# Gated convolutions ahead of the last column sums, a second norm, group choice and sort in fewer steps, and a shared down product behind the first gate-up, in a mixer and mixture-of-experts block

## What is computed

```python
mod = c @ w_ada + b_ada;  sh1, sc1, g1, sh2, sc2, g2 = split(mod, 6)      # column sums of w_ada, 1024 x 6144
h = modulate(rms_norm(x, norm_mix_g), sh1, sc1)                           # x: 256 tokens x 1024
cb, cc, cu, z, xbc, dt_raw = split(h @ w_in)
y_a = cb * causal_dwconv(cc * cu, conv_a_w)                               # the gated convolutions, 512 channels
y_b = ssd_mixer(z, xbc, dt_raw, ...)                                      # Mamba-2, 8 heads, ends in its own rms_norm
x = x + g1 * (concat([y_a, y_b]) @ w_out)
h = modulate(rms_norm(x, norm_ffn_g), sh2, sc2)                           # the second norm
scores = sigmoid(h @ w_router);  sel = scores + router_bias               # 64 experts in 8 groups of 8
# per token: a group's score is the sum of its two best; 4 groups stay; the 8 best experts in them are taken
out = (silu(h @ ws_gate) * (h @ ws_up)) @ ws_down                         # the shared expert
for e in range(64):
    out += gates[:, e:e+1] * ((silu(h @ we_gate[e]) * (h @ we_up[e])) @ we_down[e])
return rms_norm(x + g2 * out, norm_final_g)
```

## Time and profile before

| what | value |
|---|---|
| median of 3 runs | 698.68 us |
| lowest and highest | 696.64 and 699.54 us |
| the profiled execution, own time | 698.76 us |
| its span, first to last instruction | 697.0 us |
| mean granted clock of PE | 0.971 |
| PE busy | 628.4 us (90%) |
| DVE busy | 256.5 us (37%) |
| ACT busy | 124.2 us (18%) |
| moved from HBM | 248.9 MB |

### The profile page before, as it was taken

One profiled execution on the slowest core, in us unless ns is written; L12 is line 12 of the kernel. 1 busy time (PEld: TensorE's weight loads), 2 busy tenths in 40 slices (PEclk: granted clock), 3 DMA queues, 4 the chain that ended last, 5 costly groups with the idle time before them and its releaser, 6 DMA issues.

```text
span 697.0 us, 11733 instructions
## 1 busy us (share of the span) xinstructions
PE 628.4 (90%) x4453; PEld 347.2 (50%) x4453; DVE 256.5 (37%) x705; ACT 124.2 (18%) x269; POOL 43.3 (6%) x225
## 2 busy tenths in 40 slices
PE   3699999789986999999899999998899999999892
PEld 0288878534544445454344454552445455544440
DVE  0167939774374133141323231231233121432115
ACT  2311220201310111111111211110111111111113
POOL 7000000000201000001000000010000001000000
PEclk9999999969999999999999999998999999999997
DMA  8998893652429999999999999999999999999941
GB/s 345 380 402 337 332 397 135 276 223 93 181 106 415 411 423 421 422 420 418 421 421 419 421 420 421 420 421 420 420 420 419 420 421 419 420 419 422 420 207 63
DMA packets 39869, 250.75 MB, mean 360 GB/s; under 512 B 4658, under 2 KB 6786, under 8 KB 11778
## 3 DMA queue, kind: packets, MB, share of 16 engines
q1 hardware_dynamic: 38256, 248.56, 86.9%
q10 hardware_dynamic: 1554, 1.41, 0.6%
HBM read 248.91 MB, written 1.05 MB: 359 GB/s over the span
## 4 chain that ended last, share of the span: by engine, by line
PE 69%; DMA 15%; DVE 11%; ACT 2%; issue 1%; SPq 0%; ACTq 0%; DVEq 0%
DMA ring<-in_we_up_dram 11%; PE PS L1559 11%; PE PS L1555 10%; PE PS L1348 8%; PE PS L1534 8%; PE PS L1596 5%; PE PS L1565 4%; PE PS L1591 4%; DMA ring<-in_w_ada_dram 4%; PE PS L1618 3%; PE PS L1464 3%; DVE MOD L871 3%; PE PS L1614 2%; PE PS L1601 2%; DVE YLO L1184 1%
## 5 line engine op out<-in xcount | busy, mean ns | idle before, releaser
L1559 PE MATMUL PS<-ring,arena 128*64 128x256 f32 x736 | 90.0, 396 | 3.2 <-DMA ring<-in_we_up_dram 3.2
L1348 PE MATMUL PS<-hT,ring 128*128 128x256 f32 x384 | 84.7, 380 | 0.0
L1173 DVE SCALAR_TENSOR_TENSOR arena<-arena,gate,PS 128x128 f32<-128x128 f32 (+1 forms) x44 | 16.6, 378 | 178.1 <-ACT arena L795 178.1
L1348 PEld LDWEIGHTS PS<-hT,ring 128*128 128x128 f32 x384 | 72.5, 190 | 11.0 <-issue 1.5
L1555 PE MATMUL PS<-ring,arena 128*32 128x512 f32 x576 | 69.6, 635 | 3.8 <-DMA ring<-in_we_up_dram 3.8
L1184 DVE TENSOR_TENSOR YLO<-PS,YHI 128x512 fp32r<-128x512 f32 x54 | 37.3, 690 | 97.0 <-ACT YHI L806 97.0
L1534 PE MATMUL PS<-G,H2HI 128*128 128x256 f32 (+1 forms) x240 | 63.2, 299 | 9.5 <-ACT arena L786 7.0
L1559 PEld LDWEIGHTS PS<-ring,arena 128*64 128x64 f32 x736 | 51.5, 136 | 35.5 <-issue 6.6
L806 ACT CAST YHI<-PS 128x512 fp32r<-128x512 f32 x54 | 31.6, 586 | 161.5 <-PE PS L1596 79.2
L1534 PE MATMUL PS<-G,H2LO 128*128 128x256 f32 (+1 forms) x240 | 58.4, 279 | 0.0
L1534 PEld LDWEIGHTS PS<-G,H2HI 128*128 128x128 f32 x240 | 45.6, 190 | 22.1 <-issue 11.7
(11 more groups left out here) (267 smaller groups left out, 610.8 us busy)
## 6 DMA issues: line engine op xcount, KB each, us to landing
ring<-in_we_gate_dram SPq DMA_DIRECT2D x64, 1024.0 KB, 16.4
ring<-in_we_up_dram SPq DMA_DIRECT2D x64, 1024.0 KB, 19.4
ring<-in_we_down_dram SPq DMA_DIRECT2D x64, 1024.0 KB, 16.9
ring<-in_w_ada_dram SPq DMA_DIRECT2D x6, 3072.0 KB, 15.2
ring<-in_w_in_dram SPq DMA_DIRECT2D x3, 3072.0 KB, 16.0
ring<-in_w_ada_dram SPq DMA_DIRECT2D x3, 2048.0 KB, 11.2
ring<-in_w_out_dram SPq DMA_DIRECT2D x1, 3072.0 KB, 19.4
ring<-in_w_in_dram SPq DMA_DIRECT2D x1, 1568.0 KB, 27.0
```

The lines of the kernel that those rows point to most:

```text
L1348: mm = pe.matmul(PS[:, 2 + q % QB, 0:TOK], w[:, k, (m % 6) * P:(m % 6) * P + P], hT[:, k, :], start=(k == 0), stop=(k == KD - 1))
L1559: m = pe.matmul(PS[64 * c:64 * c + 64, 6, 0:FE].rearrange("p (a n) -> p a n", a=2), xt[:, k, :], gu_cols(w[0], k, c), start=(k == 0), stop ...
```

## The change

1. **Front (PE).** Block 0 of the input projection comes first and now waits for both transfers of `I 3`; the small product for `dt` stands behind it, and `dt_cols` behind block 1.
2. **Middle (DVE).** `gated_conv(2)` and `(3)` stand where `ada(7)` stood, `gated_conv(0)` and `(1)` behind the SSM part's norm, and `ada(7)` and `ada(8)` after all four.
3. **Middle (PE).** `mod_rows(4)` and `(5)` go from behind group (0, 0) to behind group (1, 0); `h2_transposes(0)` from behind (1, 0) to behind (1, 1); rows 6 and 7 from the shared product to behind the first transposes.
4. **Second norm.** X times the scale row is taken before the reciprocal root is known; one instruction then scales and shifts, with an output in plain order. The other layout is now read by PE, ACT and POOL. ACT's rounding of t = 1 stands behind the sigmoid.
5. **Group choice.** Nine instructions become seven short ones that use MAX8 and MATCH_REPLACE. `shared_hidden(0)` moves behind the mask, which is written for PE first.
6. **Sort.** Counts are read from PSUM, the rank table and the flag for overfull experts leave the path to the order; SP and POOL wait for the order alone. `shared_gate_up(0)` and `(1)` are cut in other places.
7. **Shared down product.** `shared_down(1)` goes behind `gate_up(0)`. SP loads the third expert's gate and up weights when `shared_gate_up` is done, and waits for `shared_down` only before that expert's down weights.

```diff
@@ SP
-            sp.wait_ge(order_ready, 2)
+            sp.wait_ge(order_ready, 1)
...
+                elif s == slot_of(load_no(S, 0)):
+                    sp.wait_ge(sgu_ps, TT)
...
+                    elif SLOT[q - 1] == slot_of(load_no(S, 0)):
+                        sp.wait_ge(sy_ps, TT)
@@ POOL
-                pool.tensor_tensor(H2LO[:, t, :], H2P[:, t, :], H2HI[:, t, :].bitcast(F32),
+                pool.tensor_tensor(H2LO[:, t, :].rearrange("p (k q) -> p k q", k=KD),
+                                   H2P[:, t, :].rearrange("p (q k) -> p k q", k=KD),
+                                   H2HI[:, t, :].rearrange("p (k q) -> p k q", k=KD).bitcast(F32),
                                    ALU.subtract).then_inc(h2lo_ready, 1)
...
-            pool.wait_ge(order_ready, 2)
+            pool.wait_ge(order_ready, 1)
@@ ACT
+            def high_part(t):
+                act.copy(H2HI[:, t, :].rearrange("p (k q) -> p k q", k=KD),
+                         H2P[:, t, :].rearrange("p (q k) -> p k q", k=KD)).then_inc(h2hi_ready, 1)
...
+                if t == 1:
+                    copy_mod_rows(range(6, 8))
                 act.wait_ge(h2_ready, t + 1)
                 act.wait_ge(h2T_ps, t + 1)
...
-                act.copy(H2HI[:, t, :], H2P[:, t, :]).then_inc(h2hi_ready, 1)
+                if t == 0:
+                    high_part(0)
...
+            high_part(1)
             shared_silu(0)
@@ DVE
-            ada(7)
+            gated_conv(2)
+            gated_conv(3)
             dve.wait_ge(ystd_ready, 1)
...
-            for b in (2, 3, 0, 1):
...
+            gated_conv(0)
+            gated_conv(1)
+            ada(7)
             ada(8)
...
+                link(dve.tensor_tensor(T1[:, t, :], X[:, t, :], MOD[:, 4 * D:5 * D], ALU.mult))
...
-                link(dve.scalar_tensor_tensor(out=T1[:, t, :], in0=X[:, t, :], scalar=small[:, 8 + t:9 + t],
-                                              in1=MOD[:, 4 * D:5 * D], op0=ALU.mult, op1=ALU.mult))
-                link(dve.tensor_tensor(H2P[:, t, :].rearrange("p (k q) -> p q k", k=KD),
...
+                link(dve.scalar_tensor_tensor(out=H2P[:, t, :], in0=T1[:, t, :], scalar=small[:, 8 + t:9 + t],
+                                              in1=MOD[:, 3 * D:4 * D], op0=ALU.mult, op1=ALU.add), h2_ready)
...
-            link(dve.tensor_tensor(gpair, other, mine, ALU.is_equal))
...
+            for t in range(TT):
+                link(dve.max(g8[:, t, :], gs[:, t, :]))
+            link(dve.memset(g8[:, :, TOPG:NGR], -2e30))
+            for t in range(TT):
+                link(dve.match_replace(out=grank[:, t, :], in_to_replace=g8[:, t, :], in_values=gs[:, t, :], imm_value=1e30))
+            link(dve.tensor_scalar(grank, grank, 1e30, -2e30, ALU.is_lt, ALU.mult))
...
+            link(dve.tensor_scalar(maskb, maskf, -3e30, None, ALU.is_equal), mask_ready)
             link(dve.tensor_scalar(maskf, maskf, -3e30, None, ALU.is_equal))
...
+                dve.wait_ge(order_ps, 1)
+                link(dve.tensor_scalar(order[0:1, :], PS[0:1, 2, 0:NE - FIXED], -1.0, None, ALU.add), order_ready)
+                link(dve.tensor_tensor(rankm[:], rankm[:], maskf, ALU.mult))
@@ PE
-                if q % 6 == 0 and q or q == 3:
+                if q % 6 == 0:
                     pe.wait_ge(loaded[slot_of(n)], loaded_count(n))
...
                 for k in range(KD):
+                    if q == 0:
+                        pe.wait_ge(h1_odd if k % 2 else h1_ready, k // 2 + 1)
...
                 if q == 0:
+                    dt_rows()
+                if q == 1:
                     dt_cols()
...
-                    if (t, h) == (0, 0):
+                    if (t, h) == (1, 0):
                         for r in range(4, 6):
                             mod_rows(r)
-                    if (t, h) == (1, 0):
-                        h2_transposes(0)
...
             slot_values(0)
             gate_up(0)
+            shared_down(1)
```

131 lines of the change are left out of this document (62 added, 69 removed).

## The result

| what | before | after |
|---|---|---|
| median of 20 runs each | 699.07 us | 695.06 us |
| lowest and highest | 696.22 and 701.49 us | 690.72 and 698.02 us |
| the profiled execution, own time | 698.76 us | 690.9 us |
| its span | 697.0 us | 689.1 us |
| its mean granted clock | 0.971 | 0.972 |

The ratio is 0.9934, with a 95% interval of 0.9914 to 0.9954: 4.6 us faster by the ratio, 4.0 by the medians. The forecast was 690.4, so the gain is about half of the one forecast. The profiled execution of the changed kernel took 690.9, but it is one of the two fastest of its 20; half of them took over 695. One execution of the later run e11 took 919.11, at a mean granted clock of 0.654; it counts in no ratio. So there are two questions: whether the steps of the sum hold in the profiled execution, and why most executions are 4 us slower than it.

The account below looks back on a forecast made before the run. Bound by the sorted experts' weight stream, whose end moves with its start. Middle 12.7, second norm 0.2 and routing 2.45, less front 5.4 and bubble 1.6, gain 8.35 us: 690.4, range 685.0 to 695.9.

Parts of the forecast that it names:

- a front, POOL and bubble all at their bad ends: Front, POOL's remainder in the routing and the stream's hole all at worst: time counts as same, chance 0.09.
- Front: PE's input projection: block 0 waits for the second transfer, then a low clock; loses 5.4 us (3.2 to 6.3).
- Middle: DVE's convolutions and column sums, PE's output groups: last group ends at 165.6 against 178.3, gaining 12.7 us.
- Second norm: Scaling step saves 1.95 us, ACT's square behind the rounding takes back 1.7; gains 0.2.
- rival 1: Routing: POOL's remainder slows to 3.55 from 2.37 by reading H2P with a step; 692.7 us, chance 0.2.
- Routing: From the sigmoid to the first sorted load: shorter group choice and sort, DVE held by POOL; gains 2.45 us.
- Bubble: Expert weight stream runs dry at the down load that waits for down(0); loses 1.6 us (0 to 3.7).
- rival 3: Experts' start: half clock through gate_up(0), shared_down(1) and gate_up(1), so the stream runs dry; 701 us, chance 0.03.
- (2): Front costs nothing, as the second transfer is there in time or PE's inputs are as late; 685.0 us, chance 0.12.
- (4): PE bounds the experts, so the earlier weight stream is of no use; 693 to 695 us, chance 0.05.

Follow-up runs that it names:

- e11: Changed kernel with five unread matmuls filling PE's pause ahead of the second norm's transposes of t = 1; median 692.7 us, ratio 0.9916 to the kernel before.
- e1: Changed kernel with PE waiting for the second w_in transfer at block 3 again, not block 0; median 690.52 us, ratio 0.989 to the kernel before.
- e6: Kernel before with block 0 waiting for the second w_in transfer, the dt product still ahead of it; median 699.02 us, ratio 1.0005.
- e7: Changed kernel with ada(7) ahead of the four gated convolutions again; median 699.34 us, ratio 1.0002 to the kernel before.
- e5: The changed kernel run again, unaltered; median 695.0 us, ratio 0.9935 to the kernel before; its profiled execution took 697.33.
- e4: Changed kernel with H2P written in the permuted layout again, so readers take plain order; median 690.91 us, ratio 0.9903 to the kernel before.
- e3: Changed kernel with shared_down(1) back ahead of the last gather piece; median 692.25 us, ratio 0.9919 to the kernel before.
- e8: Changed kernel with the edits of e1, e3 and e4 together; median 687.4 us, ratio 0.9827 to the kernel before.
- e10: Changed kernel with the edits of e8, plus ACT's square and root of t = 1 first; median 687.48 us, ratio 0.9824 to the kernel before.

## Why the prediction was right or wrong

**The forecast** of 690.4 fits the profiled execution (690.9), and the median, 695.06, is 4.6 above it, just inside the range's end. Faster by more than 0.5% held (0.66% by the ratio, with an interval from 0.46 to 0.86), but the gain is 4.0 to 4.6 where 8.4 was forecast. The median is in the range (to 695.9) by the range's width, and that is luck in so far as the reason is not one that the range was drawn for: a front, POOL and bubble all at their bad ends.

**Front: −4.1 in the first profile instead of −5.4, and 4.0 to 5.3 over all profiles with this front.** Block 0 did begin 3.2 later, but not all of that is the wait: PE's small transposes began 0.78 later than before (31.32 against 30.54), so by the same 1.20 the inputs would have been there at 33.6, and the wait cost 2.4. Block 0 ran at half clock and lost 1.8 by that (5.51 against 3.72), inside the bounds, though the forecast gave the long pause as the cause, and e1 shows the low clock there without it. And the `dt` product, which used to take 2.19 because it followed its inputs piece by piece, takes 1.07 behind block 0. "Nothing that PE does is left out, so the 3.2 is lost" overlooked those 1.1. e6 shows what the wait costs where the `dt` product stands ahead of it: 0.76.

**Middle: right in each link**: the root ready at 129.6 plus the front's 4.1 (133.65), `ada(8)` exposed for 7.24 (7.4), no pause ahead of the first group, 1.57 for rows 4 and 5. And e7 shows that this part carries the gain.

**Second norm: the step that was wrong, −1.4 instead of +0.2.** The forecast saw the square behind the rounding, and took that rounding as 1.06. With H2P in plain order, ACT reads it with a step of 8 values, and it takes 2.08. The forecast asked this question of POOL alone (rival 1), not of ACT, which reads the same tile in the same way. The late square then let DVE's last step fall into POOL's time, another 1.0. And one more thing was missing: the delay was entered as 1.7 us of path, while nobody asked what PE does meanwhile. It pauses 2.97 where it had paused 0.63, and in a part of the executions the clock falls behind that. In e5's profile 2.6 us went that way. The forecast priced a pause at two places, the front and `gate_up(0)`, and not here. The distance of 4 us between the median and the profiled execution is not this pause alone. The front gives up to 1.2 of it and the second fall of the clock in the routing 0.8 where it happens; how the rest is shared out, twelve single profiles don't show.

**Routing: right**, 2.4 against 2.45. One DVE instruction took 2.07 under POOL's, where DVE was expected to be held for 1.9. The held instruction was not one with two inputs, as the forecast had supposed, but a `TENSOR_SCALAR` with one.

**Bubble: right in size, wrong in place.** The forecast put it at the down load, some 35 behind the first load. It opened 19 behind the first load and ended with the load that waits for `gate_up(0)`. In the kernel before that load had this row, 17.7 behind the first; now it is 22.4 behind it.

```profile
220.82 0.34 SPq L473 DMA_DIRECT2D ring<-in_we_gate_dram  x1
```

The forecast took one margin, the tightest, and had the pause of about 3 ahead of `gate_up(0)` on paper; but it kept the half clock behind that pause for rival 3, as a case of 0.03, where 5.60 instead of 3.83 was the normal case. Its harm stayed small, since only `gate_up(0)` ran slowly and not the two products behind it.

**The rivals.** (1) POOL's remainder took 2.86, a fifth more than 2.37 and not half as much again; e4 puts the whole layout, ACT's part included, at 0.6 to 0.9 of the load. Partly so. (2) is refuted by e1. (3) came for the first of its three products only, which ran at half clock, with a hole of 2. (4) is refuted by e3, e8 and e10, whose rest is within 1 us of the kernel before's.

**Sum against what.** The execution before that was profiled was near its median, so the forecast compared like with like. But a sum over one trace forecasts an execution in which the clock falls where it fell in that trace. The kernel before spreads by 5.3 over 20 runs, the changed one, with more pauses, by 7.3, and its profiled execution was at the fast end, not near the median.

## What to carry to other kernels

Price every new pause of PE at once with the half clock that may follow it, and do so for the median, not for the one execution you have: small work that stands in a wait (here the `dt` product and `shared_down(1)`) is worth its place as filling. When a tile's layout changes, ask for the step of each of its readers, ACT's too, and which instruction stands behind the slowed one. And undo the parts of a change one at a time after it has won: three of its parts were together a loss here, and without them the same change gives 687.4 instead of 695.

## What the runs showed of the hardware

- ACT's CAST of 128x1024 fp32 takes 1.06 from a plain row and 2.08 with a step of 32 bytes between values; POOL's subtraction of the same tile 2.35 to 2.51 and 2.86 to 2.89; DVE's instruction with a write of that step 2.01 (e4) against 1.28. The Trainium skill, SBUF — State Buffer, "Door 1: The DMA port swizzle", says that accesses which cross into a new line of 16 bytes pay for it. All three rows agree with it, ACT most of all. POOL's rows show a fifth, less than the half that the page quoted in the prediction states.
- POOL's instruction holds DVE until it ends, and which DVE instruction is held is not a matter of two inputs alone: in the changed kernel it was the `TENSOR_SCALAR` with one input, 2.07 against about 0.22, while MAX8 and MATCH_REPLACE8 passed. The Trainium skill, GPSIMD Engine Reference, "Key points", names a second kind beside two inputs, instructions in a 2-port mode, which the prediction had left out. That would fit this row, but no row shows an instruction's mode.
- The same pause of 2.97 was followed by a granted clock of 0.50 in some executions and of 1.00 in another of one and the same kernel (e5 and the first profile). In the front a pause of 1.20 was followed by 0.50 in e1, e8 and e10, and by 1.00 in the kernel before. The Trainium skill, TensorE: Matmul & The Clock Gate, Part 1, says that the number of slow matmuls varies from run to run, and puts the penalty under 1% of a kernel. The 2.6 us of e5 are 0.4% of the time, which agrees; but the whole change brought no more than 0.66%.
